# Regrouping the retention products, the compressed scores and two orders of work in a two-block transformer kernel

## The reference

```python
# first block, gated linear attention, 4 heads of 128 keys and 256 values
S_t = diag(alpha_t) S_{t-1} + k_t v_t^T ; o_t = q_t S_t
# second block, sparse attention: compressed branch, 8 heads in 2 groups, 31 compressed keys
kc = compress(k_cmp, ...)            # silu(flat @ w1) @ w2
p_c = masked_softmax(einsum('bqghd,bngd->bghqn', qb, kc), m_c)
o_cmp = einsum('bghqn,bngd->bqghd', p_c, vc)      # beside a selected and a window branch
# second block, retention, 8 heads of 64
q, k = rope(q), rope(k) * 64 ** -0.5
inner = einsum('bhid,bhjd->bhij', q, k) * decay   # causal, decay by distance
o = einsum('bhij,bhjv->bhiv', inner, v)
o = (o - mean(o)) * rsqrt(var(o) + EPS) * norm_w * silu(rg)
```

## Time and profile before

| | |
|---|---|
| median of 3 runs | 2566.95 us (2566.61 to 2572.87) |
| profiled execution, its own time | 2567.48 us |
| its span, first to last instruction | 2565.6 us |
| TensorE busy | 2536.2 us, 12666 products |
| mean granted TensorE clock | 0.996 of 2.4 GHz |

### The profile page before, as it was taken

One profiled execution on the slowest core, in us unless ns is written; L12 is line 12 of the kernel. 1 busy time (PEld: TensorE's weight loads), 2 busy tenths in 40 slices (PEclk: granted clock), 3 DMA queues, 4 the chain that ended last, 5 costly groups with the idle time before them and its releaser, 6 DMA issues.

```text
span 2565.6 us, 35545 instructions
## 1 busy us (share of the span) xinstructions
PE 2536.2 (99%) x12666; PEld 2112.8 (82%) x12666; DVE 1137.4 (44%) x2238; ACT 1033.8 (40%) x1681; POOL 1049.2 (41%) x464
## 2 busy tenths in 40 slices
PE   9999999999999999999999999999999999999998
PEld 7888888887887888888889888888777678888887
DVE  7444336765444145644315544224555455322212
ACT  5222237455555234332334322224565554322321
POOL 0444454342232444544455544453123335244443
PEclk9999999999999999999999999999999999999999
DMA  7455532122222333555532554333112223233332
GB/s 298 148 191 193 189 123 85 60 81 84 98 82 83 107 98 115 188 192 190 168 124 88 198 190 145 103 125 108 50 57 78 87 82 115 66 98 98 96 102 98
DMA packets 78282, 313.11 MB, mean 122 GB/s; under 512 B 9040, under 2 KB 11728, under 8 KB 68720
## 3 DMA queue, kind: packets, MB, share of 16 engines
q1 hardware_dynamic: 65376, 238.09, 28.1%
q10 hardware_dynamic: 12816, 73.80, 8.1%
HBM read 309.72 MB, written 2.13 MB: 122 GB/s over the span
## 4 chain that ended last, share of the span: by engine, by line
PE 93%; DVE 4%; ACT 2%; issue 1%; DMA 0%; POOL 0%; DVEq 0%; ACTq 0%
PE bank L2045 26%; PE bank L2047 25%; PE bank L2046 25%; PE bank L2097 2%; PE bank L2099 2%; PE bank L2098 2%; PE bank L2480 1%; PE bank L2396 1%; PE bank L2488 1%; PE bank L2369 1%; ACT h_hi L666 0%; PE bank L2567 0%; PE pair L2560 0%; PE pair L2381 0%; DVE h_lo L1295 0%
## 5 line engine op out<-in xcount | busy, mean ns | idle before, releaser
L586 POOL TENSOR_TENSOR w_lo<-raw,w_hi 128x1024 fp32r<-128x1024 f32 x412 | 1011.1, 2456 | 1431.9 <-ACT w_hi L625 1431.8
L625 ACT ACTIVATE w_hi<-raw 128x1024 fp32r<-128x1024 f32 x420 | 443.4, 1059 | 1049.9 <-PE bank L2047 1014.4
L2045 PE MATMUL bank<-h_hi,w_hi 128*128 128x512 f32 x2064 | 819.2, 397 | 2.2 <-DVE kw_lo_b L1732 2.2
L2047 PE MATMUL bank<-h_hi,w_lo 128*128 128x512 f32 x2064 | 804.5, 390 | 0.0
L2046 PE MATMUL bank<-h_lo,w_hi 128*128 128x512 f32 x2064 | 803.8, 389 | 0.0
L2045 PEld LDWEIGHTS bank<-h_hi,w_hi 128*128 128x128 f32 x2064 | 388.3, 188 | 91.1 <-issue 12.5
L2047 PEld LDWEIGHTS bank<-h_hi,w_lo 128*128 128x128 f32 x2064 | 387.7, 188 | 82.1
L2046 PEld LDWEIGHTS bank<-h_lo,w_hi 128*128 128x128 f32 x2064 | 388.3, 188 | 77.5 <-issue 1.0
L1446 DVE TENSOR_TENSOR prod<-bank,rstd 128x512 f32<-128x512 f32 x87 | 60.1, 691 | 427.8 <-PE bank L2047 417.0
L2045 PE MATMUL bank<-act_hi,w_hi 128*128 128x512 f32 x616 | 239.6, 389 | 0.0
L2046 PE MATMUL bank<-act_lo,w_hi 128*128 128x512 f32 x616 | 239.6, 389 | 0.0
(11 more groups left out here) (484 smaller groups left out, 3103.0 us busy)
## 6 DMA issues: line engine op xcount, KB each, us to landing
raw<-slabs_dram SPq DMA_DIRECT2D x420, 512.0 KB, 3.5
adaw<-ada_dram ACTq DMA_DIRECT2D x62, 1024.0 KB, 6.8
ada<-ada_dram SPq DMA_DIRECT2D x8, 1024.0 KB, 20.3
x<-xt_dram SPq DMA_DIRECT2D x4, 512.0 KB, 5.7
adaw<-ada_dram SPq DMA_DIRECT2D x2, 1024.0 KB, 23.7
fneg<-fneg_scratch ACTq DMA_DIRECT2D x4, 512.0 KB, 3.8
sq<-fneg_scratch ACTq DMA_DIRECT2D x4, 512.0 KB, 3.8
w<-w_dram SPq DMA_DIRECT2D x1, 2048.0 KB, 8.0
```

The lines of the kernel that those rows point to most:

```text
L586: nc.gpsimd.tensor_tensor(wl[s][:], raw[s][:], wh[s][:], ALU.subtract).then_inc(lo_done, 1)
L625: nc.scalar.activation(wh[s][:], raw[s][:], ACT.Copy).then_inc(hi_done, 1)
L2045: MM(out, wh[s][:, k], a, start=first and j == 0, stop=False)
L2047: ins = MM(out, wl[s][:, k], a, start=False, stop=end and j == len(tiles) - 1)
```

## The change

In `ret_pair` the scores of blocks 0 and 1 are issued together, into four banks (blocks 1 take `TP` and `ST`); then the scores of blocks 2 and 3 with the values of block 0 (block 3 takes the second half of the banks that block 2 uses); then the values of blocks 1, 2 and 3. The fills are 14, 4, 5 and 4 where they were 12, 5, 3, 2, 2 and 3. VectorE's decay products follow; the reciprocals stand behind blocks 1 and 3; `rsq_lo` now comes ahead of `or_lo`, the remainder of the pair before. The compressed keys of both heads are laid block-diagonally into a 128 by 64 tile, and four products with 128 rows and 64 columns replace the eight. `kw_lo` is moved between the two halves of `cab`. In `gla_head` some fills of head 0 are moved.

```diff
+        def ret_bank(s, a):
+            return TB[a] if s == 1 else SC[a]
+        def ret_at(s):
+            return 2 * P if s == 3 else 0
...
-                nc.scalar.activation(kct[:, 0:NC], ST[:, 0:NC], ACT.Copy).then_inc(n_kc, 1)
+                for a in range(2):
+                    ins = nc.scalar.activation(kct[head_at(a), 32 * a:32 * a + NC], ST[head_at(a), 0:NC], ACT.Copy)
+                ins.then_inc(n_kc, 1)
...
+                V.memset(kct[:], 0.0)
...
                 for kv in range(2):
                     tile_evacuated(dve, m + kv)
+                    if kv:
+                        dve.wait_ge(n_kh, 2)
+                        for a in range(2):
+                            ins = V.tensor_tensor(kwl[a][head_at(a)], acc[m % 2][head_at(a)], kws[a][head_at(a)], ALU.subtract)
+                        ins.then_inc(acc_free[m % 2], 1)
...
-                dve.wait_ge(n_kh, 2)
-                for a in range(2):
-                    ins = V.tensor_tensor(kwl[a][head_at(a)], acc[m % 2][head_at(a)], kws[a][head_at(a)], ALU.subtract)
-                ins.then_inc(acc_free[m % 2], 1)
...
                 for n in range(8):
-                    w = T - P * (n // 2)
+                    w, at = T - P * (n // 2), ret_at(n // 2)
                     dve.wait_ge(r_s, 8 * i + n + 1)
                     if n >= 4:
-                        dve.wait_ge(r_pv, 8 * i + n - 3)
+                        dve.wait_ge(r_pv, 8 * i + n % 2 + 1)
...
-                    if behind and n in (1, 3, 5):
-                        ret_inverse(i - 1, {1: (0, 1), 3: (2,), 5: (3,)}[n])
+                    if behind and n in (3, 7):
+                        ret_inverse(i - 1, {3: (0, 1), 7: (2, 3)}[n])
                 if behind:
-                    ret_out(m, i - 1)
+                    ret_gated(m, i - 1)
                 dve.wait_ge(r_sq, i + 1)
                 V.tensor_tensor(rsql[:], rsq[:], rsqh[:], ALU.subtract).then_inc(r_sql, 1)
+                if behind:
+                    ret_out_low(i - 1)
...
                 for g in range(GROUPS - 1):
-                    for _ in range(3 if i else 2):
+                    for _ in range(3 if i or g == GROUPS - 2 else 2):
...
-                for _ in range(2 if i else 3):
+                for _ in range(2 if i else 4):
...
-                for _ in range((10, 8, 8, 3)[i]):
+                for _ in range((8, 8, 8, 3)[i]):
...
                         for t in range(TT):
-                            for a in range(2):
-                                ins = MM((SC2, TP)[a][:, 32 * t:32 * t + NC], nq[half(a), P * t:P * (t + 1)], kct[half(a), 0:NC], start=True, stop=True)
+                            ins = MM(SC2[:, 64 * t:64 * (t + 1)], nq[:, P * t:P * (t + 1)], kct[:], start=True, stop=True)
...
-                fill(12)
...
+                fill(14)
                 pe.wait_ge(r_qkl, 2 * i + 2)
+                pe.wait_ge(r_std, i)
+                scores(0)
+                scores(1)
+                fill(4)
+                pe.wait_ge(r_ad, 8 * i + 2)
+                scores(2)
+                scores(3)
                 pe.wait_ge(r_vtok, i + 1)
                 pe.wait_ge(r_ro, i)
+                values(0)
+                fill(5)
+                pe.wait_ge(r_ad, 8 * i + 4)
+                values(1)
+                pe.wait_ge(r_ad, 8 * i + 8)
+                values(2)
+                values(3)
+                fill(4)
```

More of the change, by code:

```diff
@@ L347, in build @@
         vwtok = sb("vwtok", [P, TT, P])
-        kct = sb("kct", [P, 32])
+        kct = sb("kct", [P, 64])
         vcs = sb("vc_s", [P, P], F32R)
@@ L1766, in mix2 @@
                 ret_inverse(NP - 1, range(TT))
-                ret_out(m, NP - 1)
+                ret_gated(m, NP - 1)
+                ret_out_low(NP - 1)
                 c, m = c + 4 * NP, m + 4 * NP
@@ L1822, in nsa_pair @@
                 dve.wait_ge(n_ct, i)
-                for a in range(2):
-                    ins = V.tensor_tensor(cb[:].rearrange("p (t a) j -> p t a j", a=2)[:, :, a, 0:NC],
-                                          (SC2, TP)[a][:, 0:32 * TT].rearrange("p (t j) -> p t j", j=32)[:, :, 0:NC], cmask[:], ALU.add)
-                chain.link(ins)
+                chain.link(V.tensor_tensor(cb[:].rearrange("p (t a) j -> p t a j", a=2)[:, :, :, 0:NC],
+                                           SC2[:, 0:64 * TT].rearrange("p (t a j) -> p t a j", a=2, j=32)[:, :, :, 0:NC],
+                                           cmask[:].rearrange("p t (o j) -> p t o j", o=1).to_broadcast([P, TT, 2, NC]), ALU.add))
                 chain.link(V.tensor_reduce(cm[:], valid, AX.X, ALU.max))
@@ L1898, in ret_inverse, with ret_gated @@
                     chain.link(ins)
-            def ret_out(m, i):
+            def ret_gated(m, i):
                 chain.link(V.scalar_tensor_tensor(rout[:], ro[:], rw[:, 0:1], rstd[:], ALU.mult, ALU.mult))
@@ L1904, in ret_out, with ret_out_low @@
                 V.tensor_tensor(rout[:], rout[:], rsg[:, ds(i, 1)].rearrange("p a t -> p (a t)"), ALU.mult).then_inc(r_g, 1)
+            def ret_out_low(i):
                 dve.wait_ge(r_g, i + 1)
@@ L1915, in ret_pair @@
                 for n in range(8):
-                    w = T - P * (n // 2)
+                    w, at = T - P * (n // 2), ret_at(n // 2)
                     dve.wait_ge(r_s, 8 * i + n + 1)
                     if n >= 4:
-                        dve.wait_ge(r_pv, 8 * i + n - 3)
-                    V.tensor_tensor(rad[:, n % 4, 0:w], SC[n % 2][:, 0:w], rdec[:, n % 2, 0:w], ALU.mult).then_inc(r_ad, 1)
-                    if behind and n in (1, 3, 5):
-                        ret_inverse(i - 1, {1: (0, 1), 3: (2,), 5: (3,)}[n])
+                        dve.wait_ge(r_pv, 8 * i + n % 2 + 1)
+                    V.tensor_tensor(rad[:, n % 4 if n < 4 else n % 2, at:at + w], ret_bank(n // 2, n % 2)[:, at:at + w],
+                                    rdec[:, n % 2, 0:w], ALU.mult).then_inc(r_ad, 1)
+                    if behind and n in (3, 7):
+                        ret_inverse(i - 1, {3: (0, 1), 7: (2, 3)}[n])
                 if behind:
-                    ret_out(m, i - 1)
+                    ret_gated(m, i - 1)
                 dve.wait_ge(r_sq, i + 1)
                 V.tensor_tensor(rsql[:], rsq[:], rsqh[:], ALU.subtract).then_inc(r_sql, 1)
+                if behind:
+                    ret_out_low(i - 1)
                 if ahead:
@@ L2547, in fill, with scores @@
                         next(filler, None)
-                fill(12)
-                pe.wait_ge(r_qkl, 2 * i + 2)
+                def scores(s):
+                    at = ret_at(s)
+                    for z, (k, q) in enumerate(((rqkh, rqkh), (rqkh, rqkl), (rqkl, rqkh))):
+                        for a in range(2):
+                            h = slice(64 * a, 64 * (a + 1))
+                            ins = MM(ret_bank(s, a)[:, at:at + T - P * s], k[h, 1, P * s:P * (s + 1)], q[h, 0, P * s:T],
+                                     start=z == 0, stop=z == 2)
+                            if z == 2:
+                                ins.then_inc(r_s, 1)
@@ new lines, in values @@
+                def values(j):
+                    at = ret_at(j)
+                    for a in range(2):
+                        h = slice(64 * a, 64 * (a + 1))
+                        MM(OV[h, P * j:T], rvtok[:, j, h], rad[:, 2 + a if j == 1 else a, at:at + T - P * j], start=j == 0,
+                           stop=j == TT - 1, skip_group_check=True).then_inc(r_pv, 1)
+                fill(14)
+                pe.wait_ge(r_qkl, 2 * i + 2)
+                pe.wait_ge(r_std, i)
+                scores(0)
@@ L2569, in ret_pair @@
-                fill(3)
+                values(0)
[6 more added lines that the diff above has]
+                fill(4)
                 pe.wait_ge(r_in, 48)
```

## The result

| | before | changed |
|---|---|---|
| median (runs beside each other) | 2566.95 us, 5 runs | 2552.01 us, 5 runs (2550.28 to 2556.52) |
| profiled execution, its own time | 2567.48 us | 2555.18 us |
| its span | 2565.6 us | 2553.5 us |
| mean granted TensorE clock in it | 0.996 | 0.994 |

What follows compares the result with a forecast made beforehand. TensorE, busy 2536.2 of 2565.6 us, was taken as the bound. Terms 2.3 + 0.7 + 1.7 + 0.8 + 4.7 + 1.2 + 3.6 = 15.0 us off 2567.5 gave 2552.5, 2552 for the median; range 2549.5 to 2557.

Steps and rivals of the forecast that it cites:

- Retention, grouping: Retention: joined scores and values and fewer returns to the stream save 1.17 us a pair, 4.7 us in four pairs.
- Retention, waits: Retention: TensorE's waits on `rqk_lo` (1.2 us) and `rsq_lo` (3.6 us) go.
- Start of the second mixer: Start of the second mixer: TensorE's wait on `kw_lo` goes, 2.3 us less.
- Compressed scores: Sparse attention: four merged products for eight save 0.27 us in each of three pairs, 0.8 us, bounds 0 and 1.1.
- Head 0, fills: Linear attention, head 0: TensorE does one fill more before the operands it waits for, 0.7 us less.
- Head 0, the clock: Linear attention, head 0: the granted clock stays up behind the shorter waits, 1.7 us less, bounds 0 and 1.7.
- Grouping by returns alone: Rival, retention: grouping saves only the returns to the stream, total 2555.1 us; chance 0.13.
- `rsq_lo` late: Rival, retention: VectorE still reaches `rsq_lo` late and its three waits of 3.6 us return, total 2555.6 us; chance 0.12.
- the slower case: Rival, retention: TensorE waits for the values of blocks 2 and 3 in every pair, total 2570 us; chance 0.03.
- The compressed scores did not cost what they did: Rival, sparse attention: the four merged products cost as much as the old eight, total 2552.8 us; chance 0.07.
- The rival of the clock: Rival, linear attention, head 0: the clock falls again, 1.7 us more, total 2553.7 us; chance 0.2.

Runs made afterwards that it cites:

- Experiments 6 and 11: 6: changed kernel with the values of blocks 1, 2 and 3 apart, 2555.1 us; 11: changed kernel with the scores of blocks 0 and 1 apart, 2554.39 us.
- experiment 5: Changed kernel with `or_lo` again ahead of `rsq_lo` on VectorE, grouping as changed; 2554.1 us median.
- experiment 1: Changed kernel with retention alone put back to its old form; 2561.92 us median, ratio 0.9979 to the kernel before.
- experiment 8: Changed kernel with 12 fills ahead of a pair's first scores and 6 behind its last values, for 14 and 4; 2553.22 us median.
- experiment 2: Changed kernel with `kw_lo` again behind all eight `cab` operations; 2556.61 us median.
- experiment 3: Changed kernel with the old fills of head 0 in the linear attention; 2554.43 us median.
- experiment 9: Changed kernel once more, unaltered, with its own profile; 2553.03 us median, ratio 0.994 to the kernel before.

## Why the prediction was right, and where it was not

The prediction was 2552 us, its range 2549.5 to 2557, and 2552.01 was measured. By its own steps:

**Retention, grouping: 4.7 us.** Shown. The rows after give 0.19 (block 1) + 0.19 (blocks 2 and 3) + 0.35 (values) + 0.40 (returns) = 1.13 us a pair, 4.5 in four. The values were 0.42 in the step and are 0.35; block 3 was 0.14 and is 0.19. Experiments 6 and 11 undo two parts, 0.75 and 0.40 us a pair.

**Retention, waits: 4.8 us.** 9.5 us of the stretch less 4.5 leaves 5.0. `rsq_lo` is shown by experiment 5 and the waits' absence: the order gives 1.7 us of it, the fill the rest. `rqk_lo` was right in kind and is about right in size for these two traces, but half of its longest wait hung on a late DMA. Where the DMA wasn't late, experiment 1's two waits are 0.6 us for 1.1, and experiment 8 gives 0.3 us for two of the fills where the step said 1.2.

**Start of the second mixer: 2.3 us.** Shown by experiment 2's wait of 2.2 us, and 2.1 us in the stretch.

**Compressed scores: 0.8 us.** Shown: 0.84 and 0.89 us in the stretch, nothing in pair 0. The four products take 0.85 us where the step had 0.89. The rule of the Trainium skill that the step weighed ("TensorE: Matmul & The Clock Gate", section "Why this matters for your kernels", small-K matmuls) would have given nothing. The measurement decides against it for this size: eight products of 64 rows and 31 columns, two at once, take 1.03 us, more than four of 128 rows and 64 columns (0.85), and they have the changes of array around them. That is the Trainium skill's own point elsewhere: "TensorEngine Tiling (Array Packing)" (section "Tiling Modes", key properties) says that a change of the tiling mode drains TensorE. The 0.20 us at each return in experiments 6 and 11 agree with it, and so does their absence behind the compression.

**Head 0, fills: 0.7 us.** Shown by experiment 3, 0.73. The step had 1.8 us of waits left; experiment 9 has 1.4, as the added fill is the ninth, which stands 0.3 us for its accumulator. That changes nothing behind it, since VectorE sets when the cross products start.

**Head 0, the clock: 1.7 us. This step failed.** It took the fall behind the waits of 1.31 and 1.15 us as their effect, and one fill more as its cure. Experiment 3 has the old fills, the same 0.96 us of work in the same stretch and no fall; experiment 2 has the changed fills and 1.92 us of work, and the fall is there. The reason given, that the longer `kw_lo` wait had no fall behind it, fell too: in experiment 2 it had one. In the changed kernel's first trace head 0 did keep its clock, but the same trace had the lower clock elsewhere, twice for 6.8 us in the first 34 us, where the trace before has it twice for 3.4 us. Of the thirteen traces two have the fall in head 0: one of the two with the old fills, and one of the nine with the changed ones. The two with the fills further ahead have none. So the fills alone don't decide it; whether they make it rarer, so few traces can't tell. The falls come and go with the execution, and the times go with them: in ten runs of the changed kernel the span is 2548.6 us at a mean clock of 0.997, 2549.3 to 2551.4 at 0.996, and 2553.4 to 2554.9 at 0.994.

So the sum was 15.0 us with a term of 1.7 that was not shown to be the change's, and what the stages show is 0.7 + 2.1 + 0.8 + 9.5 = 13.1 us. The medians moved by 14.9 and, with experiment 9 beside its own runs of the kernel before (2568.61), by 15.6. Two parts of the difference can be read from these last runs. The time outside the span, from first to last instruction, is 2.4 us for the kernel before and 1.7 for the changed one: 0.7 us that no stage contains. And the mean granted clock is 0.9947 over the nine runs of the one and 0.9952 over the five of the other. Fitted over 29 runs of the kernel before, 0.001 of clock goes with 1.3 us of span, and over ten of the changed one with 1.7, so this is some 0.8 us, an estimate. Some 1 us stays open, and so does the cause of the 0.7 us. That 2552.01 hit 2552 is in this measure luck.

**The rivals.** Grouping by returns alone, `rsq_lo` late and the slower case did not come: the decay products kept 2.4 us to spare. The compressed scores did not cost what they did. The rival of the clock was the truer picture, though not as one outcome: the clock falls in some executions with either set of fills.

## What to carry to other kernels

Where TensorE is busy 99% of the time and small products of half arrays are woven into a full-array stream, count the changes of array as instructions: each return from half arrays cost 0.20 us, each entry about as much, and joining groups paid half of what retention gained, a third of this change. A wait on VectorE is best cut by asking what stands ahead of the awaited operation and waits for a third engine. Before a fall of the clock in one trace becomes a term, look for it in a second trace of the same kernel.

## What the runs showed of the hardware

The granted clock fell from 2.4 to 1.2 GHz behind waits of 1.3 to 2.5 us in sum in some executions and not in others of nearly the same program: at head 0 in two of the eleven traces with such waits and not in the others, at `kw_lo` (2.2 us) in experiment 2 and not before. A full-array product behind a group of half-array products took 0.43 us in the chain, 0.25 behind a group of full-array products, and 0.23 in the stream. Four float32 products of 128 rows and 64 columns (0.85 us) were cheaper than eight of 64 rows and 31 columns that run two at once (1.03 us).
